# Loading the eleventh weight piece of each expert phase in quarters, three of them ahead of the first gather

## The reference, cut to what matters

```python
def expert_choice_moe(x, w_router, b_router, w_gate, w_up, w_down):
    b, s, d = x.shape
    cap = CAPACITY_FACTOR * s // N_EXPERTS              # 64 tokens for each of 16 experts
    logits = jnp.einsum('bsd,de->bse', x, w_router) + b_router
    aff = jax.nn.softmax(logits, axis=-1)
    gate, idx = lax.top_k(aff.transpose(0, 2, 1), cap)
    xs = x[bidx, idx]                                   # the gather of rows
    hid = jax.nn.silu(jnp.einsum('becd,edf->becf', xs, w_gate)) * jnp.einsum('becd,edf->becf', xs, w_up)
    ys = jnp.einsum('becf,efd->becd', hid, w_down) * gate[..., None]
    return jnp.zeros_like(x).at[bidx, idx].add(ys)
```

## Time and profile before

| What | Value |
| --- | --- |
| median of 3 runs | 2523.14 us (2521.2 to 2523.38) |
| time of the profiled execution | 2521.9 us |
| its span in the trace | 2519.8 us |
| mean granted clock of TensorE | 0.994 |
| PE busy | 2442.7 us, 97% |
| DVE, ACT, POOL busy | 49%, 18%, 5% |
| read from HBM | 597 MB, 240 GB/s over the span |

### The profile page before, as it was taken

The page is one execution under the profiler, slowest core; times in us unless marked ns, Lnnn a source line. Parts: engine busy times, 40 slices in busy tenths (PEclk is TensorE's granted clock), DMA queues, the critical chain, the costliest instruction groups (busy, mean ns, idle before and its releaser), DMA issues.

```text
span 2519.8 us, 26913 instructions
## 1 busy us (share of the span) xinstructions
PE 2442.7 (97%) x10855; PEld 1523.6 (60%) x10855; DVE 1229.2 (49%) x2148; ACT 462.0 (18%) x986; POOL 123.2 (5%) x204
## 2 busy tenths in 40 slices
PE   8999999999999999999999999889999999999899
PEld 4458888888888888786653333333576553333333
DVE  4667898755766554556741222111756641121112
ACT  3432121002322100324610000000125510000000
POOL 1301110000000000001100000000001000000000
PEclk9999999999999999999999999999999999999999
DMA  8635775551443324313159999999431359999998
GB/s 310 213 109 182 269 245 161 159 145 39 134 134 109 92 67 118 117 65 134 68 213 387 428 427 427 427 428 419 147 123 76 125 195 426 426 427 427 427 428 355
DMA packets 189595, 605.38 MB, mean 240 GB/s; under 512 B 10416, under 2 KB 124544, under 8 KB 164384
## 3 DMA queue, kind: packets, MB, share of 16 engines
q1 hardware_dynamic: 172592, 548.46, 56.4%
q0 software_dynamic: 15584, 50.95, 5.9%
q10 hardware_dynamic: 1296, 4.25, 0.4%
HBM read 597.34 MB, written 6.29 MB: 240 GB/s over the span
## 4 chain that ended last, share of the span: by engine, by line
PE 79%; DMA 15%; DVE 3%; SPq 1%; issue 1%; ACT 1%; DVEq 0%; ACTq 0%
DMA arena<-in_w_down 14%; PE ps L2320 11%; PE ps L2928 10%; PE ps L2445 7%; PE ps L2968 7%; PE ps L2331 6%; PE ps L2827 4%; PE ps L2645 4%; PE ps L2289 4%; PE ps L2605 3%; PE ps L2236 2%; PE ps L2356 2%; PE ps L2214 2%; PE ps L2979 2%; PE ps L2762 1%; PE ps L2563 1%
## 5 line engine op out<-in xcount | busy, mean ns | idle before, releaser
L2320 PE MATMUL ps<-arena 128*128 128x256 f32 x1280 | 278.0, 379 | 0.0
L2320 PEld LDWEIGHTS ps<-arena 128*128 128x128 f32 x1280 | 242.5, 190 | 33.7 <-issue 1.1
L2928 PE MATMUL ps<-arena,first 128*64 128x512 f32 x1024 | 231.4, 593 | 10.3 <-DMA arena<-in_w_up 10.3
L2928 PE MATMUL ps<-arena 128*64 128x512 f32 x1024 | 233.7, 598 | 0.5 <-DMA arena<-in_w_up 0.3
L2968 PE MATMUL ps<-arena 128*64 128x512 f32 x892 | 207.0, 620 | 24.7 <-DMA arena<-in_w_down 23.4
L2445 PE MATMUL ps<-arena 128*128 128x256 f32 x896 | 193.8, 379 | 0.1
L2445 PEld LDWEIGHTS ps<-arena 128*128 128x128 f32 x896 | 170.1, 190 | 23.6 <-issue 0.5
L2928 PEld LDWEIGHTS ps<-arena,first 128*64 128x64 f32 x1024 | 73.2, 137 | 159.7 <-issue 137.3
L2968 PEld LDWEIGHTS ps<-arena 128*64 128x64 f32 x892 | 67.3, 142 | 161.6 <-issue 159.8
L2928 PEld LDWEIGHTS ps<-arena 128*64 128x64 f32 x1024 | 73.7, 137 | 139.5 <-issue 131.9
L2331 PE MATMUL ps<-arena 128*128 128x256 f32 x672 | 146.0, 379 | 0.0
(11 more groups left out here) (491 smaller groups left out, 3245.3 us busy)
## 6 DMA issues: line engine op xcount, KB each, us to landing
arena<-in_w_gate SPq DMA_DIRECT2D x64, 2048.0 KB, 36.3
arena<-in_w_up SPq DMA_DIRECT2D x64, 2048.0 KB, 35.1
arena<-in_w_down SPq DMA_DIRECT2D x54, 2048.0 KB, 34.3
arena<-in_ffn_w SPq DMA_DIRECT2D x24, 2048.0 KB, 10.1
arena<-in_w_mod POOLq DMA_DIRECT2D x80, 512.0 KB, 5.0
arena<-in_ffn_w SPq DMA_DIRECT2D x32, 1024.0 KB, 7.5
arena<-in_w_in SPq DMA_DIRECT2D x10, 1536.0 KB, 10.3
arena<-in_w_down SPq DMA_DIRECT2D x12, 1024.0 KB, 37.9
```

Of the source, the lines that this page charges most:

```text
L2320: ins = mm(ps[:, i % 6, 0:256], src[:, k, P * j:P * j + P], x[:, k, :], start=(k == 0), stop=(k == 3))
L2928: ins = mm(ps[CAP * half:CAP * half + CAP, bank, :], xsT[q][:, k, CAP * (e % 2):CAP * (e % 2) + CAP], wv[:, k, 512 * half:512 * half + 512 ...
```

## The change

Piece 10 is no longer one DMA but four, one for each k: 1024 of the 4096 elements of each partition, rows of 4 KB. All four wait for `xn_saved` as before. Only the last waits for the first gather too. The counts of landings of buffer 9 become three higher. What is loaded, and where to, stays the same, as does everything behind piece 10.

```diff
@@ -381,10 +381,10 @@
             return (s, l * uses + k + (more_uses if k else 0), l * uses + k + 1 + more_uses,
-                    16 * (l * (R2_LANDS[s] + total) + R2_LANDS[s] + k + 1 + (more_lands if k else 0)))
+                    16 * (l * (R2_LANDS[s] + total) + R2_LANDS[s] + k + 1 + (more_lands if k else 0) + (QUARTERS - 1 if s == ORDER[10] else 0)))
 
         def slot_total(s):
-            return loads_before(s, LOADS) + (PARTS_11 - 1 if s == ORDER[0] else 0)
+            return loads_before(s, LOADS) + (PARTS_11 - 1 if s == ORDER[0] else QUARTERS - 1 if s == ORDER[10] else 0)
@@ -511,10 +511,14 @@
                         sp.wait_ge(sm[name], value)
-                        if s == 9:
-                            sp.wait_ge(got[0], 16 * (8 * l + 1))
                     w = a[("w_gate_2", "w_up_2", "w_down_2")[part // 2]][l, e]
                     half = w[512 * (part % 2):512 * (part % 2) + 512, :]
+                    if n == 10:
+                        for k in range(QUARTERS):
+                            if k == QUARTERS - 1:
+                                sp.wait_ge(got[0], 16 * (8 * l + 1))
+                            sp.dma_start(ring2[s][:, 1024 * k:1024 * k + 1024], half.rearrange("(p k) n -> p k n", k=4)[:, k, :]).then_inc(r2_in[s], 16)
+                        return
```

## The result

The changed kernel takes 2529.36 us in the median (2527.66 to 2530.91, 10 runs) against 2521.84 us before (10 runs, 2518.59 to 2523.38): 7.5 us slower, a ratio of 1.0028 with an interval of 1.0019 to 1.0037. The forecast was 2522.8 us in a range that ended at 2526.3.

The account below looks back on a forecast made before the run. Each expert phase was taken to end with its unbroken weight stream, PE not being the only bound. Gain 2 x 0.8 = 1.6 us less gather delay 1.3 gave 0.3 us shorter: 2522.8 us, range 2520.0 to 2526.3.

Parts of the forecast that it names:

- step 3: First gather of each layer: quarters ahead delay its landing by 1.0 and 0.3 us, together 1.3, bounds 0 and 1.9.
- What bounds a phase: Expert phases: the gapless weight stream (426 GB/s) sets the end; every delay of the gather costs its full size.
- Step 1: SP queue: three quarters go when the copy of the rows lands, 1321.6 to 1322.4 us, in layer 1 from about 2066.1.
- step 2: DMA engines ahead of the gather: idle, so three quarters land at 1327.9 us, in layer 1 at 2072.4.
- The reading of rows 10: A later gather, issued at 1344.65 beside weights, took 10.6 us: a gather lands when weights issued ahead have landed.
- The Trainium skill's rule: Engines alternate queues by whole packets: gather waits at most about one quarter's share, 1.2 us per layer; sum 0.8 us slower.
- Step 5: Small parts: three more DMA issues per layer, 4 KB rows and higher semaphore counts cost nothing.
- Step 4: Weight stream behind the gather: only piece 12's backlog is gained, 0.8 us per layer of 3.69, bounds 0.4 and 0.8.
- The clock: Rival: PE's longer wait drops its clock in the first matmuls, 1.7 us per layer; at most 3.7 us slower, 2526.8; 14%.
- a gather held up like the later ones and further falls: Slow side past 5 us: gather held up 10.6 us, or more clock drops than one per layer; chance 0.04.
- The cases with a name: Forecast within 1.5 us of old time 60%, clock drop 14%, full stream shift 5%, undisturbed gather 15%, change not acting 6%.
- The signs of being wrong: In the trace: gather over 5.5 us, clock under 1.0 between 1328 and 1336, or stream end over 2 us earlier.

Follow-up runs that it names:

- the kernel with 21 multiplications: Changed kernel with 21 instead of 7 multiplications of constants on PE ahead of the wait for the first gather: 2528.82 us against 2522.48 before.
- split alone: Kernel before with piece 10 loaded in four quarters, all four behind the first gather: 2522.26 us against 2521.86, ratio 1.0002.
- the changed kernel with 13 multiplications: Changed kernel with 13 instead of 7 multiplications of constants on PE ahead of the first gather: 2528.86 us against 2521.86 before, ratio 1.0027.

## Why the prediction was wrong, point by point

One more window of the kernel before, while only gathered rows and no weights move; the point on step 3 rests on it (columns as in rows 3). The engines are busy for 0.67 of the time at 162 GB/s.

```profile
1325.00:1327.00 2.00, 1.74 (x9) 1.19 (x7) 0.00 (x0) 0.00 (x0) 1.51 (x2) 1.00 0.67 162
```

- **What bounds a phase: right.** Its stream of weights ends it, and what delays its head is paid one to one (the kernel with 21 multiplications).
- **Step 1, when the quarters go: nearly right.** Forecast 1.9 us ahead of the gather in layer 0 and 2.8 in layer 1; measured 1.2 and 2.4. The copy of the rows took 11.9 us instead of 11.2. The other kernels with the same quarters ahead had 1.8 to 2.0 in layer 0, so this is scatter, but it cost layer 0 about 1 us.
- **Step 3, the gather's delay: the term that failed.** Taken at 1.3 us for both layers together with an upper bound of 1.9; measured 3.68 + 2.45 = 6.1. I had added the gather's own data behind the quarters at the stream's rate, 0.26 MB in 0.6 us, and let it land when it was moved. But the rows showed more: with the engines quiet until 1325 the gather landed at 1327.26, so from its first possible packet to its landing it needs 2.3 us with no weights beside it. The window above says that the rows don't move at the stream's rate either. Put behind the quarters' data, which I estimate to end at 1327.0 (0.9 us ahead of step 2's landing at 1327.9), the gather lands at 1329.3, a delay of 2.0 us and not 0.7 to 1.3. The quarters were late as well: in the kernel with 21 multiplications, where they went at 1321.47, almost as forecast, the last of them landed at about 1329.0 and the gather at 1329.9. The gathers at the forecast lead of 1.9 to 2.0 us took 6.4 and 6.5 us, a delay of 2.7. For the rest the slow rate of gathered rows, 203 GB/s at a share of 0.96 in the changed kernel, where I had put 426, is the likely reason; no run isolates it. In layer 1 I let the quarters land just ahead of the old landing and called that free; what moves beside the gather slows it, as the kernel with the quarters behind the gather's issue shows, and not only what lands before it. There the measured delay is 2.45 us.
- **The reading of rows 10** (a gather lands with the weights issued ahead of it) came from one pair and is no rule to price by: with the quarters issued behind it, the gather is still held up by 1.8 to 2.2 us.
- **The Trainium skill's rule** (DMA: Bandwidth & Descriptors, "Queues, rings and completion order": whole packets in turn, by which I estimated 1.2 us per layer) put the sign of the sum right, 0.8 us slower, and the size well short of 3.68 and 2.45 us. That the gather is slowed by weights issued behind it (5.5 and 6.0 us) agrees with turns between queues.
- **Step 5, the small parts: right.** The split alone costs nothing that can be told.
- **Step 4, the gain: wrong.** 0.8 us per layer was forecast; with three quarters never loaded it is 421.0 us from piece 12 to the end where before had 421.1. A backlog of that kind is real in the landings (piece 12 took 7.9 us in layer 1 and 7.4 in layer 0 instead of 8.3) and gone by the seventh piece. The 7.5 us of rows 9 were not those of quiet engines, as I had them: from 1302 to 1306 the engines of before were busy for 0.63 and 0.67 of the time. I checked one later issue for slack (piece 15), and took an engine share of 1.01 over 410 us as proof that nothing more could be lost; a mean over 410 us doesn't show a loss of 1 us. Which engines run dry, and where, stays open.
- **The clock: priced right, weighed wrong.** The rival said 1.7 us per layer, if the clock falls before piece 12 is released; measured 1.7 and 1.5 us (15.66 and 15.44 us for 64 matmuls against 13.95). I gave it 14%, since layer 1 of before had waited 1.01 us without a fall. But that reasoned from the idleness of my too small delay: with the 4.33 and 3.46 us that came, it fell in both layers. One statement there was false: that the fall at 1346 in layer 0 of before "is not critical now". The table above prices it at 1.5 us, and it is the 1.5 us by which layer 0 was the longer phase in before (434.9 against 433.4).
- **The sum with the measured terms:** delay 3.7 + 2.4, fall 1.7 + 1.5, gain 0, less the 1.5 us of the fall that layer 0 had before: 7.8 us, against 7.7 in the traces and 7.5 in the medians.
- **The chances:** a gather held up like the later ones and further falls got 0.04 together. They depend on each other, since a longer wait makes a fall more likely in these traces, and I had priced them as if apart. The cases with a name already summed to 1.00, so this 0.04 had no room in them.
- **The signs of being wrong** were well chosen: a gather of over 5.5 us and a clock under 1.0 between 1328 and 1336 both came.

## What to carry to other kernels

Before a transfer is moved ahead of a small gather that everything waits for, price the gather as a transfer of its own. A first estimate is the time that it needs on quiet engines, added to all that may move beside it, and not its bytes over the stream's rate. Ask also what the first late instruction does to PE's clock; a microsecond of waiting at the head of a phase can cost a second one in the matmuls behind it. And test what the move can bring at most, by leaving the transfer out, before its cost is argued: here the traces show nothing, and the medians leave room for 2.3 us at most.

## What the runs showed of the hardware that was not expected

- A gather of 64 rows of 4 KB, beside or behind 1.57 MB of weights, took 5.3 to 7.4 us instead of 3.7 to 4.0. Weights issued 0.35 to 0.67 us behind it slowed it as well (6.0 and 5.5 us).
- While gathered rows moved, the engines were busy for 0.96 of the time at 203 GB/s in the changed kernel, and for 0.67 at 162 GB/s in the kernel before; in the windows of weights they gave 426 at a share of 1.01.
- The granted clock fell to 0.50 after waits of PE as short as 0.69 us (ahead of the first w_down matmuls, layer 0, split alone), 0.94 and 1.10 us, and not after others of 0.94 and 1.12; in the changed kernel's layer 1 it stayed at 1.00 through 3.46 us of idleness and fell 0.9 us behind its end. A fall avoided at one wait came back at the next in the changed kernel with 13 multiplications. After waits of 1.8 us and more at the head of a phase it fell every time. What decides in the short cases stays open.
